# A gated delta rule over the prompt: the order of v's convolution, its third projection unit and the splits of the q and k weights

## The reference, cut to what matters

```python
qkv, new_conv = causal_conv(concatenate([q_a, k_a, v_a]), conv_buf, conv_w)   # 4 taps per channel
q, k, v = split(silu(qkv))
q = l2norm(q) * DK ** -0.5
k = l2norm(k)
decay = where(causal, exp(gc_i - gc_j), 0)            # gc: running sum of log decay
A  = where(strict, (beta * k) @ k.T * decay, 0)
u, w = solve(A + I, [v * beta, k * beta * exp(gc)])   # unit lower triangular
qk = (q @ k.T) * decay
for each chunk:  v_new = u - w @ S;  o = q_dec @ S + qk @ v_new;  S = S * g_end + k_dec.T @ v_new
```

## Time and profile before

| | |
|---|---|
| median of 3 runs | 3031.47 us (3029.08 to 3031.53) |
| the profiled execution | 3034.24 us, its span 3032.6 us |
| PE busy | 2419.7 us, 80% |
| DVE busy | 1593.2 us, 53% |
| ACT busy | 1093.2 us, 36% |
| POOL busy | 424.0 us, 14% |
| DMA | 444.55 MB, mean 147 GB/s |

### The profile page before, as it was taken

One profiled execution on the slowest core, in us unless ns is written; L12 is line 12 of the kernel. 1 busy time (PEld: TensorE's weight loads), 2 busy tenths in 40 slices (PEclk: granted clock), 3 DMA queues, 4 the chain that ended last, 5 costly groups with the idle time before them and its releaser, 6 DMA issues. The chain is left out here.

```text
span 3032.6 us, 36285 instructions
## 1 busy us (share of the span) xinstructions
PE 2419.7 (80%) x12823; PEld 1934.2 (64%) x12824; DVE 1593.2 (53%) x2056; ACT 1093.2 (36%) x1557; POOL 424.0 (14%) x442
## 2 busy tenths in 40 slices
PE   4689888898865756789996989887937999999940
PEld 2478877887754633644445989883425888888710
DVE  2356456645663211124445464633346899999805
ACT  3234323332331100013333333321115777777702
POOL 1022012201240120012222000000012111111003
PEclk8889999999987757589997999998968999999965
DMA  7411112110202123031105545444246999999625
GB/s 285 169 38 44 49 26 59 45 53 20 59 16 91 35 83 128 1 84 42 41 0 188 149 122 150 121 129 161 85 175 248 401 406 404 405 403 402 258 104 187
DMA packets 316737, 444.55 MB, mean 147 GB/s; under 512 B 56626, under 2 KB 254786, under 8 KB 296883
## 3 DMA queue, kind: packets, MB, share of 16 engines
q1 hardware_dynamic: 292508, 379.32, 35.5%
q0 software_dynamic: 11168, 39.12, 3.6%
q10 hardware_dynamic: 13000, 25.30, 2.2%
HBM read 388.59 MB, written 57.14 MB: 147 GB/s over the span
## 5 line engine op out<-in xcount | busy, mean ns | idle before, releaser
L2504 DVE TENSOR_TENSOR ex_w_r<-ex_w,ex_wh 128x2048 fp32r<-128x2048 f32 x192 | 433.2, 2285 | 59.7 <-ACT ex_wh L2446 59.6
L2446 ACT ACTIVATE ex_wh<-ex_w 128x2048 fp32r<-128x2048 f32 x192 | 367.6, 1917 | 130.8 <-PEq L2153 43.2
L1866 PE MATMUL mg_psum<-mg_xl,mg_wh 128*128 128x352 f32 x768 | 252.1, 328 | 0.0
L1926 DVE TENSOR_TENSOR mg_w_r<-mg_w,mg_wh 128x1024 fp32r<-128x1024 f32 x96 | 131.6, 1375 | 122.7 <-ACT mg_wh L1879 122.4
L1879 ACT ACTIVATE mg_wh<-mg_w 128x1024 fp32r<-128x1024 f32 x96 | 101.4, 1056 | 184.1 <-DVE mg_out L1953 123.6
L2038 PE MATMUL op_mix<-op_w,op_mT 128*128 128x512 f32 x288 | 131.1, 615 | 25.0 <-DMA op_w<-in_w_out_dram 25.0
L923 PE MATMUL gd_x<-gd_Y,gd_am 128*128 128x128 f32 x256 | 50.0, 358 | 124.9 <-DMA gd_YT<-yt_block_scratch 83.0
L1866 PEld LDWEIGHTS mg_psum<-mg_xl,mg_wh 128*128 128x128 f32 x768 | 148.2, 193 | 0.0
L1866 PE MATMUL mg_psum<-hT_r,mg_wh 128*128 128x352 f32 x384 | 127.2, 331 | 18.4 <-DVE mg_w_r L1926 18.4
L902 PE MATMUL gd_ps<-gd_hh,gd_wh 128*128 128x352 f32 x368 | 121.4, 330 | 10.6 <-DVE gd_w_r L769 9.9
L923 PEld LDWEIGHTS gd_x<-gd_Y,gd_am 128*128 128x128 f32 x256 | 43.6, 258 | 130.6 <-issue 129.6
(11 more groups left out here) (617 smaller groups left out, 5987.5 us busy)
## 6 DMA issues: line engine op xcount, KB each, us to landing
ex_w<-in_w_gate_dram SPq DMA_DIRECT2D x64, 1024.0 KB, 7.9
ex_w<-in_w_up_dram SPq DMA_DIRECT2D x64, 1024.0 KB, 7.3
ex_w<-in_w_down_dram SPq DMA_DIRECT2D x64, 1024.0 KB, 8.2
ada_w<-in_w_ada_dram SPq DMA_DIRECT2D x24, 1024.0 KB, 15.3
mg_w<-in_w_in_dram SPq DMA_DIRECT2D x48, 512.0 KB, 3.6
gd_w<-in_w_in_dram SPq DMA_DIRECT2D x32, 512.0 KB, 4.2
expert_out_scratch<-ex_y ACTq DMA_DIRECT2D x32, 512.0 KB, 7.7
mg_w<-in_w_br_gdn_dram SPq DMA_DIRECT2D x24, 512.0 KB, 3.9
```

The source lines that it names most:

```text
L1866: last = nc.tensor.matmul(pm[b][q][:, 0:R], a, x, start=(m == 0 and v == 0), stop=(m == KD - 1 and v == 2))
L1926: nc.vector.tensor_tensor(wl_r[q][:], wl[q][:], wh[q][:].bitcast(F32), ALU.subtract).then_inc(w_low, 1)
L2446: nc.scalar.activation(wh[at][:], wl[b][u][:], ACT.Copy).then_inc(w_high, 1)
L2504: nc.vector.tensor_tensor(wl_r[b][u][:], wl[b][u][:], wh[at][:].bitcast(F32), ALU.subtract).then_inc(w_low, 1)
```

## The change

Four pieces are moved; no instruction is added or taken away.

- ACT: `high(0, i + 1)`, the high half of q's next weight tile, goes from ahead of the Ln and Exp pairs to a place between the moves of v's second and third unit.
- DVE: `low(0, i + 1)` goes from ahead of the norm products to behind the scaled scores. Of `conv(2, i, ..)` only the taps 0 and 1 stay ahead of `low(1, i + 1)` and `solve(i)`; taps 2 and 3 go behind the solve, ahead of the wait for the tanh.
- PE: `project(2, 2, ..)`, v's third unit, goes from ahead of the scores to behind them.

The one-line summary of the change also speaks of GpSimd masks right behind the scaled scores; the diff holds no line of GpSimd's queue, whose masks already wait for `ats` alone.

```diff
--- before.py
+++ after.py
@@ -659,8 +659,6 @@
                     for g in range(2):
                         act.wait_ge(capped, i * 8 + g * 4 + 4)
                         nc.scalar.activation(DT[g][:], E[g][:], ACT.Exp).then_inc(dt, 1)
-                    if nxt:
-                        high(0, i + 1)
                     for t in range(2):
                         for g in range(2):
                             n = i * 4 + t * 2 + g + 1
@@ -671,6 +669,8 @@
                             act.wait_ge(logged, n)
                             nc.scalar.activation(th[t][:, g * C4:(g + 1) * C4], th[t][:, g * C4:(g + 1) * C4], ACT.Exp, scale=-0.5).then_inc(rooted, 1)
                     evac(2, 1, i)
+                    if nxt:
+                        high(0, i + 1)
                     evac(2, 2, i)
                     if nxt:
                         high(1, i + 1)
@@ -800,8 +800,6 @@
                         for n in range(4):
                             at = slice(n * P, (n + 1) * P)
                             nc.vector.tensor_scalar(E[g][:, at], pp[g][:, at], col(GC, 4 * g + n), 0.0, ALU.subtract, ALU.min).then_inc(capped, 1)
-                    if nxt:
-                        low(0, i + 1)
                     for t in range(2):
                         for g in range(2):
                             at = slice(g * C4, (g + 1) * C4)
@@ -817,10 +815,13 @@
                             at = slice(n * P, (n + 1) * P)
                             nc.vector.scalar_tensor_tensor(AT[g][:, at], X[g][0][:, at], col(BETA, 4 * g + n), DT[g][:, at], ALU.mult, ALU.mult).then_inc(ats, 1)
                         nc.vector.tensor_tensor(qkm[g][:], X[g][1][:], DT[g][:], ALU.mult).then_inc(qds, 1)
-                    conv(2, i, 0, CONV)
+                    if nxt:
+                        low(0, i + 1)
+                    conv(2, i, 0, 2)
                     if nxt:
                         low(1, i + 1)
                     solve(i)
+                    conv(2, i, 2, CONV)
                     dve.wait_ge(v_tanh, i + 1)
                     nc.vector.scalar_tensor_tensor(y[2][:], th[2][:], 1.0, y[2][:], ALU.add, ALU.mult).then_inc(v_silu, 1)
                     if nxt:
@@ -953,8 +954,6 @@
                             nc.tensor.matmul(X[g][t][:], c.ones[:], th[t][:, g * C4:(g + 1) * C4], start=True, stop=True).then_inc(summed, 1)
                     for half in range(2):
                         project(2, 1, half, i)
-                    for half in range(2):
-                        project(2, 2, half, i)
                     pe.wait_ge(normed, i * 4 + 4)
                     for g in range(2):
                         for n in range(4):
@@ -965,6 +964,8 @@
                             at = slice((4 * g + n) * P, (4 * g + n + 1) * P)
                             last = nc.tensor.matmul(X[g][1][:, n * P:(n + 1) * P], y[1][:, at], y[0][:, at], start=True, stop=True)
                         last.then_inc(scored, 1)
+                    for half in range(2):
+                        project(2, 2, half, i)
                     if nxt:
                         pe.wait_ge(v_evac, i * 3 + 3)
                         for half in range(2):
```

## The result

The changed kernel takes 3012.8 us, the kernel before 3031.5 us, the ratio 0.9938 with a 95% interval of 0.9921 to 0.9955: 19 us less, where 14.7 were forecast. The profiled execution took 3014.99 us, its span is 3013.4 us.

The account below looks back on a forecast made before the run. Bound: a head's path through norms, scores, scaled scores, DRAM round trips and block solve, then PE alone. Gain 3.0 - 1.4 = 1.6 us a head, 11.2 in seven, plus 3.5 in the last: 14.7 off 3031.5, 3017 us, range 3002 to 3029.

Parts of the forecast that it names:

- parts 1 and 2: ACT and PE ahead of the scores: norm products and scores 2.1 us earlier, only if both moves are made together.
- S: End of the block solve on DVE in the followed head: 402.52 us before, forecast 399.5, 3.0 us earlier.
- part 3: SP's queue: v's weight load goes out ahead of the scaled scores' stores, so the blocks land 2.6 us later, near 390.2.
- part 4: DVE: two taps leave the solve's front; POOL's k products hold its start to near 392.2, its end 3.0 us earlier.
- part 5: PE behind the solve: k's first unit waits for taps, tanh and q's moves; levels at S + 8.7, not 7.3, costing 1.4 us.
- the clock's loss: PE at half clock behind its gap: 3.3 us lost a head, moved from the levels to k's unit, unchanged in size.
- A: Rival: POOL's lock is not in the solve's way; 3.5 us a head, 28 us in all, 3003 us; chance 0.15.
- B: Rival: gains cancel, S moves only 2 us or k's unit begins cold; 0 to 0.6 us a head, 3027 us; chance 0.20.
- C: Rival: SP's load ahead of the stores delays the blocks beyond 393.8, making the kernel slower, 3043 us; chance 0.12.
- D: Rival: the diff does not do what it says, touching nothing of GpSimd's masks; worth zero, no chance given.

Follow-up runs that it names:

- e6: Kernel before with only the moves of q's next weights' high half (ACT) and low half (DVE, ahead of the whole convolution): 3038.8 us.
- e7: Kernel before with only v's third unit moved behind the scores on PE: 3039.8 us.
- e2: Kernel before with only the split of v's convolution, taps 2 and 3 behind the solve: 3017.6 us.
- e3: Changed kernel with SP's load of v's next weights put behind the stores of the scaled scores: 3006.4 us.
- e5: Changed kernel with POOL's k products, and its joins of hT in the last head, held back until v's silu is done: 2979.1 us.
- e10: Changed kernel with 44 matmuls that nobody reads filling PE's gap ahead of k's first unit: 2993.6 us.
- e11: Kernel before with 64 matmuls that nobody reads filling PE's gap ahead of the levels: 3026.4 us.
- e12: Kernel before with v's convolution split (taps 2 and 3 behind the solve) and POOL's k products held back until v's silu: 2976.5 us.
- e1: Changed kernel with v's convolution left whole ahead of the solve, the other moves kept: 3017.1 us.
- e4: Changed kernel with ACT's moves of q's second and third unit and z's high weight half ahead of v's tanh: 3009.4 us.
- e8: Changed kernel with load behind the stores, q's moves ahead of v's tanh and POOL's k products behind v's silu, all three: 2967.6 us.

## Why the prediction was right, point by point

- **The earlier scores** (parts 1 and 2): right to 0.1 us. First Ln 368.45 for 368.5, scores 374.29 for 374.35, scaled scores done 2.1 us earlier, PE idle 1.79 us for 1.85. e6 and e7 show that each move alone brings nothing, and that it costs 8 to 9 us, which the prediction had not priced. Beside the split they bring little: e2 has the same S without them.
- **SP's load ahead of the stores** (part 3): issue at 382.15 for 382.1, the blocks' load at 387.63 for 387.5, the first step at 390.33 for 390.2. The stores' landing goes from 2.3 to 4.3 us, and back in e3. So both stores are down between the prediction's two bounds (385.3 and 388.6). The trace does not contradict the order within a ring that the prediction cites from the Trainium skill's page "DMA: Bandwidth & Descriptors", section on queues, rings and completion order, but the blocks are there 1 us ahead of the late end that it was said to give (391.3), and no run here tells such an order from a plain sharing of the transfer.
- **The solve and POOL** (part 4): DVE ready at 388.3 for 388 (its bound of 8 us behind 381.1 would be 389.1; the passes took 7.3), POOL's k products from 388.4 to 392.4 for 388.0 to 392.0. S forecast at 399.5, found at 395.68 + 3.55 = 399.23, against 402.52. Mean over six heads: 2.6 us earlier, where 3.0 were forecast; the 0.4 us are the two heads in which the clock fell ahead of the scores, not foreseen. e3 and e5 show what POOL's instructions cost the solve, at both ends: 10.6 us for the solve with four POOL instructions in it, 7.36 with none. That agrees with the exclusive lock that the Trainium skill's page "SBUF — State Buffer", section "SBUF: two separate sides", states.
- **The tail of the convolution** (part 5): PE's start at S + 4.55 for S + 4.6, and at full clock the levels at S + 8.5 for S + 8.7 (e10). But the price of the part was put at 1.4 us and is 0.4: S to the next head is 42.40 to 97.94, 55.5 us, against 55.2 before. The term that was mis-sized is the clock's loss, "the same 3.3 us" on both sides. Before it is 1.3 us (47.8 against 46.5 in e11's undisturbed heads), since the rest of it hid the second group's transfer, for which the changed kernel does not wait at all any more; after it is 2.0 us (10.5 against e10's 8.5). So 1.2 us for the order (8.5 against 7.3), 0.7 for the clock and 1.4 back for the transfer (46.5 against 45.06), which comes to the measured 0.4 within 0.1 us.
- **The sum**: 2.6 - 0.4 = 2.2 us a head for 1.6, and 4.1 us in the last head for 3.5. That makes 19.5 in place of 14.7 and explains the whole difference. Two of the errors pull against each other, S too early by 0.4 us and part 5 too dear by 1.0, and that the sum hides part of both is luck.
- **The rivals**: A falls with e3. B's cold clock is there, but it costs 0.7 us a head more than before and not the whole gain. C's mechanism is there in full, with the blocks 2.6 us later, but most of that passes while DVE is still busy or would have taken turns with POOL: DVE idles 2.0 us for the blocks, and without the delay (e3) S comes only 0.5 us earlier. D is true of the diff and worth nothing: POOL's first mask starts 0.1 us behind the first group's scaled scores in both traces.

## What to carry to other kernels

When a step moves in one queue, follow what waits for it in all others: here a projection moved behind the scores pulled a 512 KB load in front of the stores of the path, and e12, in which the scores come later, ends its solve 1.7 us earlier than e5. Look for GpSimd work beside a chain of short dependent VectorE steps: here each step that met a GpSimd instruction took as long as that instruction, and one wait that kept them apart was worth 34 us, nearly twice the change itself. And the low clock behind a gap may hide a transfer, so that keeping the clock high brings less than the time at the low clock suggests (1.3 us a head in e11, where 2.7 were expected).

## What the runs showed of the hardware

- A step of 0.2 us on DVE took about 1 us beside POOL instructions of 1.04 us (e3), and 2.34 us beside those of 2.37 us (last head of the changed kernel), one POOL instruction to each step: there 26.7 us for a solve of 7.3.
- TensorE's clock can fall behind idling as short as 1.8 us, and does not always: it went to 1.2 GHz in the fourth and seventh heads of the changed kernel, while the four others from the second on, with the same idling, kept 2.4 GHz. Over the changed kernel, e1, e3, e4, e5, e8 and e10, which all idle 1.8 us ahead of the scores, it fell there in 7 of 42 heads; behind the 3.7 to 3.9 us of e7 in all six. In e8 it fell in all six behind waits of 0.6 us and of at most 2.5 us, and in e11 in two of six behind two waits of 1.0 to 1.4 us.
- Two 256 KB stores issued right behind a 512 KB load on SP's queue landed in 4.3 us instead of 2.3; a 64 KB load issued 0.7 us behind such a load (e3) took 3.5 us instead of 2.7.
